# Modulation vectors: which engine multiplies and sums the gates' and the shifts' weight pieces

## The chip, the cores and the metric

One core of a Trainium2 chip runs the whole network. It has a matrix engine (TensorE, PE), a vector engine (VectorE, DVE), an activation engine (ScalarE, ACT), a general engine (GpSimd, POOL) and a queue that issues the DMAs (SyncE, SP). The metric is the device time of one execution in microseconds (us).

## The reference

Three kinds of layer follow one another: a hybrid attention layer with a dense feed-forward, a state-space layer (Mamba) with a mixture of experts, and two attention layers of a second block. Six times the normed activations are modulated by a vector that is computed from a conditioning vector `c` of 1024 numbers:

```
def adaln(c, w, b):
    mod = jax.nn.silu(c) @ w + b
    shift, scale, gate = jnp.split(mod[:, None, :], 3, axis=-1)
    return shift, scale, gate

def modulate(x, norm_w, shift, scale):
    return rmsnorm(x, norm_w) * (1 + scale) + shift
```

Each `w` is 1024 x 3072 in float32, 12.6 MB. The shift and the scale are needed at the layer's norm, the gate only at the layer's end, where it multiplies what is added to the residual.

## The kernel before

**The stream.** All weights come from memory in chunks of at most 128x1024 float32 (512 KB), through a ring of six buffers (`RING`). The DMA queue fills buffer c % 6 when chunk c-6 has been used up. There are two kinds of chunk. A *half* is a piece of a matrix that TensorE multiplies: ScalarE rounds it (line 507), VectorE subtracts the rounded part from the raw one (line 519, both inputs in SBUF), and TensorE takes three products of high and low parts (lines 530 to 532); the ring buffer is free after VectorE's subtraction. A *piece* belongs to a modulation: 24 of them for each of the six, `step` 0 to 15 (even ones the shift's, odd ones the scale's columns) and `gate` 16 to 23.

**What is done with a piece.** VectorE multiplies it by silu(c), one number for each partition, and adds it to the accumulator `macc`, 128x1024 for each of shift, scale and gate: the first piece of each with one product (line 580), the others with a product and a sum in one instruction (line 583). The ring buffer is free after it. When all pieces of a vector are summed, TensorE sums the partitions with matmuls against a matrix of ones (`mod{i}.sum` after step 15, `mod{i}.gates` after gate 23), and VectorE adds the bias (lines 589 to 603). Of modulation 0, TensorE multiplies pieces 9 and 10 directly (`DIRECT`), so that VectorE does 142 of the 144.

**What sets the order.** Every engine's instructions stand in an order written out by hand. The list `Stream.back` gives the pieces' order; `back_steps` and `back_until` take the next entries of it between the halves, at the same places of VectorE's and TensorE's programs. Modulation 0 runs at the very start, its gates and modulation 1 in the hybrid layer (one piece after each half), modulations 2, 3 and most of 4 in the dense feed-forward and the first part of the Mamba layer; then there is a pause (`BACK_PAUSE`) through the experts, and the last gates of 4 and all of 5 come in the first layer of the second block. Semaphore counts are found by a rehearsal of the same programs, and named: `mod1.step23` is the event that gate piece 23 of modulation 1 is in the sum. GpSimd does nothing.

Of the kernel before, what the change touches and what calls it, by code (L numbers as in the profile page):

```python
# [12 lines left out]
ALU = mybir.AluOpType  # L13
# [3 lines left out]
D = 1024  # L17
T = 256
NT = 2
KD = 8  # L20
# [46 lines left out]
class Ledger:  # L67
# [8 lines left out]
    def tick(self, sem, name, by=1):  # L76
        n = self.reached.get(sem.name, 0) + by
        self.reached[sem.name] = n
        self.brought[name] = (sem, n)
        return sem, by  # L80

    def when(self, name):
        return (None, 1) if self.known is None else self.known[name]
# [19 lines left out]
class Banks:  # L103
# [35 lines left out]
SEMAPHORES = (  # L139
    "params_landed", "x_landed", "x_scaled", "tables_landed", "start_landed", "raw_landed0", "raw_landed1", "raw_landed2", "raw_landed3", "raw_landed4", "raw_landed5",  # L140
    "half_rounded", "half_split", "half_used", "vector_step", "scalar_step",
    "mod_stepped", "mod_summed", "mod_ready", "small_split",
    "squared", "weighted", "norm_scaled", "norm_rooted", "norm_turned", "norm_filled_a", "norm_filled_v", "h_rounded", "h_split",
    "row_spread", "row_copied", "mix_turned", "mix_rounded", "mix_split", "added",
    "proj_out_a", "proj_out_v", "proj_turned",
# [318 lines left out]
def landed(k, key):  # L464

    c = k.stream.chunk_of[key]
    return k.landed[c % RING], 16 * (c // RING + 1), k.ring[c % RING]
# [5 lines left out]
def on_sync(sp, k):  # L473

    S, d = k.S, k.d
    sp.dma_start(k.par[:, :], d["par"]).then_inc(S.params_landed, 16)
    sp.dma_start(k.X[:, :, :], d["x"].rearrange("(t p) n -> p t n", p=128)).then_inc(S.x_landed, 16)
    for c, (src, width, freed) in enumerate(k.stream.chunks):
        if c == RING:
            sp.dma_start(k.cst[:, 0:512], d["cst"][:, 0:512]).then_inc(S.tables_landed, 16)  # L480
        if c == 2 * KD + RING:
            for dst, src_ in ((k.cst[:, 512:], d["cst"][:, 512:]), (k.small[:, :], d["small"]), (k.postok[:, :], d["pos"]),
                              (k.dtw[:, :, :], d["dtw"])):
                sp.dma_start(dst, src_).then_inc(S.start_landed, 16)
        if c == k.stream.chunk_of["half", k.stream.first["second0"]] + SPLITS + RING:
            over_sync(sp, k)
        if c >= RING:
            sp.wait_ge(*k.when(k.stream.chunks[c - RING][2]))
        sp.dma_start(k.ring[c % RING][:, 0:width], src).then_inc(k.landed[c % RING], 16)
    for t in range(NT):  # L490
        for c in range(2):
            sp.wait_ge(*k.when(f"s1.added{2 * t + c}"))
            sp.dma_start(k.out[t * 128:(t + 1) * 128, c * 512:(c + 1) * 512], k.X[:, t, c * 512:(c + 1) * 512]).then_inc(S.out_landed, 16)
    sp.wait_ge(S.out_landed, 64)
# [40 lines left out]
def mm(pe, out, a, b, start=True, stop=True):  # L535
    return pe.matmul(out, a, b, start=start, stop=stop, skip_group_check=True)  # L536
# [11 lines left out]
def mod_col(i):  # L548
    return 16 + (8 if i >= 4 else 0)
# [4 lines left out]
DIRECT = (10, 9)  # L554


def back_vector(v, k):

    if k.at_back["vector"] == len(k.stream.back):
        return  # L560
    kind, i, r = k.stream.back[k.at_back["vector"]]
    k.at_back["vector"] += 1
    if kind in ("rest", "shift"):
        return
    S, tick, when = k.S, k.tick, k.when
    mod, bias = k.d["mod"][i], k.V[f"b{i}"]
    if kind in ("step", "gate"):
        k.stream.ask(("mod", i, r), mod[r], QUARTER, f"mod{i}.step{r}")
        if i == 0 and r in DIRECT:
            return  # L570
        sem, value, w = landed(k, ("mod", i, r))
        n, part, before = (r // 2, r % 2, r - 2) if kind == "step" else (r - 2 * KD, 2, r - 1)
        if i == 0 and before in DIRECT:
            before -= 2
        c = k.st[:, mod_col(i) + n:mod_col(i) + n + 1]
        m = k.macc[:, part * D:(part + 1) * D]
        v.wait_ge(sem, value)
        if n == 0:
            v.wait_ge(*when("c.silu" if i == 0 else f"mod{i - 1}.sum" if kind == "step" else f"mod{i - 1}.gates"))
            v.tensor_scalar(m, w[:, :], c, None, ALU.mult).then_inc(*tick(S.mod_stepped, f"mod{i}.step{r}"))  # L580
        else:
            v.wait_ge(*when(f"mod{i}.step{before}"))
            v.scalar_tensor_tensor(out=m, in0=w[:, :], scalar=c, in1=m, op0=ALU.mult, op1=ALU.add).then_inc(*tick(S.mod_stepped, f"mod{i}.step{r}"))  # L583
    elif kind == "sum":
        bank = k.banks[k.bank_of.get(f"mod{i}.sum", 0)]
        m = k.mods[:, i, 8:16]
        if i == 0:
            v.wait_ge(*when(f"mod0.step{DIRECT[-1]}"))
            v.tensor_tensor(k.mods[:, 0, 0:16], k.banks[k.bank_of.get("mod0.direct", 0)][:, 0:16], bias[:, 0:16], ALU.add).then_inc(*tick(S.mod_ready, "mod0.biased"))
            v.wait_ge(*when("mod0.biased"))  # L590
            bias = k.mods[:, 0, :]
        v.wait_ge(*when(f"mod{i}.sum"))
        v.tensor_tensor(k.mods[:, i, 0:16], bank[:, 0:16], bias[:, 0:16], ALU.add).then_inc(*tick(S.mod_ready, f"mod{i}.summed"))
        v.wait_ge(*when(f"mod{i}.summed"))
        v.scalar_tensor_tensor(out=m, in0=m, scalar=1.0, in1=k.V[f"n{i}"], op0=ALU.add, op1=ALU.mult).then_inc(*tick(S.mod_ready, f"mod{i}.ready"))
    else:
        bank = k.banks[k.bank_of.get(f"mod{i}.gates", 0)]
        m = k.mods[:, i, 16:24]
        v.wait_ge(*when(f"mod{i}.gates"))
        v.tensor_tensor(m, bank[:, 16:24], bias[:, 16:24], ALU.add).then_inc(*tick(S.mod_ready, f"mod{i}.{'gated' if i < 4 else 'biased'}"))  # L600
        if i >= 4:
            v.wait_ge(*when(f"mod{i}.biased"))
            v.tensor_tensor(m, m, k.V[f"post{i - 4}"], ALU.mult).then_inc(*tick(S.mod_ready, f"mod{i}.gated"))


def back_tensor(pe, k):
    if k.at_back["tensor"] == len(k.stream.back):
        return
    kind, i, r = k.stream.back[k.at_back["tensor"]]
    k.at_back["tensor"] += 1  # L610
    if i == 0 and kind == "step" and r in DIRECT:
        direct_tensor(pe, k, r)
    if kind in ("step", "gate", "rest"):
        return
    if i == 0 and kind in ("shift", "sum"):
        first_sum_tensor(pe, k, kind)
        return
    lo, hi, steps = (0, 16, f"mod{i}.step15") if kind == "sum" else (16, 24, f"mod{i}.step23")
    bank = k.back_banks.borrow(pe, f"mod{i}.{kind}" if kind == "sum" else f"mod{i}.gates", f"mod{i}.summed" if kind == "sum" else f"mod{i}.gated")
    pe.wait_ge(*k.when(steps))  # L620
    for j in range(lo, hi):
        last = mm(pe, bank[:, j:j + 128], k.macc[:, j * 128:(j + 1) * 128], k.C["ones"])
    last.then_inc(*k.tick(k.S.mod_summed, f"mod{i}.sum" if kind == "sum" else f"mod{i}.gates"))
# [267 lines left out]
def square(a, k, name, t, c, into):  # L891

    a.activation(into, k.X[:, t, c * 512:(c + 1) * 512], ACT.Square,
                 accum_out=k.st[:, 56 + 2 * t + c:57 + 2 * t + c]).then_inc(*k.tick(k.S.squared, f"{name}.squared{2 * t + c}"))
# [2487 lines left out]
def on_scalar(a, k):  # L3382
    S, tick, when = k.S, k.tick, k.when
    a.wait_ge(S.params_landed, 16)
    a.activation(k.st[:, 0:16], k.par[:, 0:16], ACT.Exp, scale=-1.0).then_inc(*tick(S.scalar_step, "c.exp"))
    a.wait_ge(S.x_landed, 16)
    for t in range(NT):
        for c in range(2):
            if t == 1:
                a.wait_ge(*when(f"x.squared{c}"))  # L3390
            square(a, k, "x", t, c, k.arena[:, c * 512:(c + 1) * 512])
    hybrid_scalar(a, k)
    dense_scalar(a, k)
    mamba_scalar(a, k)
    moe_scalar(a, k)
    final_scalar(a, k)
    for l in range(2):
        second_scalar(a, k, l)


def model(nc, d, out):
    with ExitStack() as ctx:
        k = Kernel(nc, ctx, d, out)
        k.start_over()
        for program in (on_vector, on_scalar, on_tensor, on_sync):
            program(Rehearsal(), k)
        k.ledger.close()
        k.start_over()
        with nc.Block() as block:
            block.tensor(lambda e: on_tensor(e, k))  # L3410
            block.vector(lambda e: on_vector(e, k))
            block.scalar(lambda e: on_scalar(e, k))
            block.sync(lambda e: on_sync(e, k))


# [145 lines left out]
```

## Time and profile before

| | |
|---|---|
| median of 3 runs | 2034.95 us (2033.78 to 2046.62) |
| profiled execution, its own time | 2032.43 us |
| span of its trace | 2030.7 us |
| TensorE busy | 96% of the span |
| VectorE busy | 1701.1 us (84%) |
| ScalarE busy | 1323.5 us (65%) |
| GpSimd busy | 0.2 us |
| moved by DMA | 560 MB, mean 276 GB/s |

The busy share of TensorE is that of overlapping, modelled spans: it says when the engine had work, not that it ran at its peak. "Waits" name the engine and line that stood still, the one that released it, the sum in us, how often and the longest.

### The profile page before, as it was taken

The page shows a single profiled execution, that of the slowest core. Times are in us where ns is not written, and L with a number is a line of the kernel's source. Part 1 is how long each engine was busy: PE and PEld are TensorE (multiplying, and loading weights), DVE is VectorE, ACT ScalarE, POOL GpSimd, SP SyncE. Part 2 cuts the span into 40 slices and gives each one's busy share as a digit, 9 for nine tenths or more (in the row PEclk, how much of TensorE's full clock was granted, in tenths as well). Part 3 has the DMA queues.
Part 4 walks back from the last instruction along what each step waited for, and adds up shares of the span by engine and source line. Part 5 has one row for each costly group of instructions (what it writes and reads, how often), then busy time and mean ns, then how long its engine had stood idle before and what let it go on. Part 6 is the DMA issues. An engine that isn't in the chain of part 4 may idle for free.

```text
span 2030.7 us, 28448 instructions
## 1 busy us (share of the span) xinstructions
PE 1951.6 (96%) x10304; PEld 1630.0 (80%) x10304; DVE 1701.1 (84%) x2491; ACT 1323.5 (65%) x1976; POOL 0.2 (0%) x4
## 2 busy tenths in 40 slices
PE   6898999998998999999999999999999998999997
PEld 5777889978977788788888878888888786787886
DVE  7797878768886698989989899898989998986864
ACT  4453544355674687778888787887878785455553
POOL 0000000000000000000000000000000000000000
PEclk9998999999999999999999999999999999999999
DMA  9856689845332298989989899898999994873630
GB/s 371 311 193 232 244 300 329 285 146 193 142 111 98 104 376 326 365 327 387 366 338 374 323 367 382 330 368 328 374 359 351 353 387 157 291 250 114 229 131 25
DMA packets 154211, 560.20 MB, mean 276 GB/s; under 512 B 17232, under 2 KB 17488, under 8 KB 153936
## 3 DMA queue, kind: packets, MB, share of 16 engines
q1 hardware_dynamic: 154064, 558.30, 74.8%
q8 instruction: 85, 1.39, 0.3%
q14 instruction: 62, 0.51, 0.1%
HBM read 557.18 MB, written 1.05 MB: 275 GB/s over the span
## 4 chain that ended last, share of the span: by engine, by line
PE 80%; DVE 10%; ACT 5%; issue 3%; DMA 2%; SPq 0%; DVEq 0%; ACTq 0%
PE ps L530 22%; PE ps L532 22%; PE ps L531 22%; PE ps L536 10%; PE ps L540 3%; DVE spl L519 2%; DVE macc L583 2%; ACT sph L507 2%; DMA ring<-in_mod 1%; DMA ring<-in_hyb_w_in 1%; DVE arena L2177 1%; DMA ring<-in_dense_down 1%; ACT arena L774 1%; ACT arena L2143 1%; DVE hL L887 0%
## 5 line engine op out<-in xcount | busy, mean ns | idle before, releaser
L519 DVE TENSOR_TENSOR spl<-ring,sph 128x1024 fp32r<-128x1024 f32 x906 | 1076.4, 1217 | 185.5 <-ACT sph L507 173.1
L507 ACT ACTIVATE sph<-ring 128x1024 fp32r<-128x1024 f32 x906 | 948.5, 1058 | 392.5 <-PE ps L532 214.3
L530 PE MATMUL ps<-sph,hH 128*128 128x512 f32 (+1 forms) x1296 | 518.2, 400 | 2.5 <-DVE hL L887 1.3
L532 PE MATMUL ps<-sph,hL 128*128 128x512 f32 (+1 forms) x1296 | 505.2, 390 | 0.0
L531 PE MATMUL ps<-spl,hH 128*128 128x512 f32 (+1 forms) x1296 | 504.1, 389 | 0.0
L530 PEld LDWEIGHTS ps<-sph,hH 128*128 128x128 f32 x1296 | 244.0, 188 | 52.2 <-issue 3.8
L532 PEld LDWEIGHTS ps<-sph,hL 128*128 128x128 f32 x1296 | 243.5, 188 | 51.6
L531 PEld LDWEIGHTS ps<-spl,hH 128*128 128x128 f32 x1296 | 244.1, 188 | 47.7 <-issue 1.0
L530 PE MATMUL ps<-sph,rH 128*128 128x512 f32 x664 | 268.4, 404 | 4.2 <-DVE rL L1237 3.2
L532 PE MATMUL ps<-sph,rL 128*128 128x512 f32 x664 | 259.9, 391 | 0.0
L531 PE MATMUL ps<-spl,rH 128*128 128x512 f32 x664 | 259.3, 391 | 0.0
L530 PE MATMUL ps<-hH,sph 128*128 128x256 f32 x640 | 186.3, 291 | 5.9 <-DVE arena L1193 4.0
L531 PE MATMUL ps<-hL,sph 128*128 128x256 f32 x640 | 183.4, 287 | 0.0
L532 PE MATMUL ps<-hH,spl 128*128 128x256 f32 x640 | 183.3, 286 | 0.0
L583 DVE SCALAR_TENSOR_TENSOR macc<-ring,st,macc 128x1024 f32<-128x1024 f32 x124 | 158.1, 1278 | 3.5 <-DMA ring<-in_mod 2.3
L530 PEld LDWEIGHTS ps<-sph,rH 128*128 128x128 f32 x664 | 125.1, 188 | 32.4 <-DVE rL L1237 4.0
L536 PE MATMUL ps<-arena 128*128 128x128 f32 (+6 forms) x828 | 137.6, 307 | 9.8 <-DVE arena L2336 7.1
L532 PEld LDWEIGHTS ps<-sph,rL 128*128 128x128 f32 x664 | 124.9, 188 | 27.3
L531 PEld LDWEIGHTS ps<-spl,rH 128*128 128x128 f32 x664 | 125.4, 189 | 24.7 <-issue 1.0
L540 PEld LDWEIGHTS ps<-cst,arena 128*128 128x128 f32 (+1 forms) x636 | 82.8, 145 | 67.0 <-issue 34.1
L530 PEld LDWEIGHTS ps<-hH,sph 128*128 128x128 f32 x640 | 125.3, 196 | 8.6 <-DVE arena L1193 4.2
L540 PE MATMUL ps<-cst,arena 128*128 128x128 f32 (+1 forms) x636 | 109.9, 281 | 22.2 <-ACT arena L2161 5.5
(316 smaller groups left out, 1702.6 us busy)
## 6 DMA issues: line engine op xcount, KB each, us to landing
ring<-in_moe_gu SPq DMA_DIRECT2D x448, 512.0 KB, 5.3
ring<-in_moe_down SPq DMA_DIRECT2D x224, 512.0 KB, 5.3
ring<-in_mod SPq DMA_DIRECT2D x144, 512.0 KB, 5.2
ring<-in_w_in SPq DMA_DIRECT2D x64, 512.0 KB, 4.4
ring<-in_dense_gu SPq DMA_DIRECT2D x44, 512.0 KB, 5.3
ring<-in_ssm_w_in SPq DMA_DIRECT2D x40, 512.0 KB, 3.8
ring<-in_dense_down SPq DMA_DIRECT2D x22, 512.0 KB, 5.5
ring<-in_hyb_w_in SPq DMA_DIRECT2D x20, 512.0 KB, 5.7
```

The lines of the kernel that those rows point to most:

```text
L507: a.activation(k.high[m % SPLITS][:, 0:w], raw[:, 0:w], ACT.Copy).then_inc(k.S.half_rounded, 1)
L519: v.tensor_tensor(k.low[m % SPLITS][:, 0:w], raw[:, 0:w], k.high[m % SPLITS][:, 0:w], ALU.subtract).then_inc(*k.tick(k.S.half_split, f"hal ...
L530: pe.matmul(out, a[0], b[0], start=start, stop=False, skip_group_check=True)
L531: pe.matmul(out, a[0], b[1], start=False, stop=False, skip_group_check=True)
L532: return pe.matmul(out, a[1], b[0], start=False, stop=stop, skip_group_check=True)
L536: return pe.matmul(out, a, b, start=start, stop=stop, skip_group_check=True)
L540: return pe.transpose(out, in_, k.C["ident"][0:n, 0:n])
L583: v.scalar_tensor_tensor(out=m, in0=w[:, :], scalar=c, in1=m, op0=ALU.mult, op1=ALU.add).then_inc(*tick(S.mod_stepped, f"mod{i}.step{r}"))
L774: a.activation(k.norm_space.fulls[2 * t + h][:, j, :], bank[:, j * 128:(j + 1) * 128], ACT.Identity, bias=k.mods[:, i, c:c + 1], scale=k.m ...
L2143: a.activation(conv_slot(k, f), bank, ACT.Identity, bias=k.V["convb"][:, f:f + 1], scale=cw[:, f, 3:4]).then_inc(*tick(S.conv_in, f"ssm{j} ...
L2177: v.scalar_tensor_tensor(out=dst, in0=M.raw[m % 6][:, n:n + T], scalar=cw[:, f, n:n + 1], in1=dst, op0=ALU.mult, op1=ALU.add).then_inc(*ti ...
```

## The change

GpSimd gets a program of its own. It takes the gates' pieces of all six modulations (48) and, from modulation 1 on, the shifts' pieces (the even steps, 40): 88 of the 142 that VectorE did. VectorE keeps modulation 0's steps and all scales. For the first piece of a vector GpSimd does one product into `macc`; for each of the others a product in place in the ring buffer, a wait for that product and for the sum before, and a sum into `macc`. The ring buffer is free after the sum. TensorE's matmuls for `mod{i}.sum` wait for the last shift piece as well as for the last scale piece. The pieces' order, the ring and TensorE's program are otherwise the same.

```
+def pooled(kind, i, r):
+
+    return kind == "gate" or kind == "step" and i > 0 and r % 2 == 0
+
+
+def back_pool(g, k, i, r):
...
+    c, m = k.st[:, mod_col(i) + n:mod_col(i) + n + 1], k.macc[:, part * D:(part + 1) * D]
+    g.wait_ge(sem, value)
+    if n == 0:
+        g.wait_ge(*when("c.silu" if i == 0 else f"mod{i - 1}.sum" if kind == "step" else f"mod{i - 1}.gates"))
...
+        g.tensor_scalar(m, w[:, :], c, None, ALU.mult).then_inc(*tick(S.mod_pooled, f"mod{i}.step{r}"))
+        return
+    g.tensor_scalar(w[:, :], w[:, :], c, None, ALU.mult).then_inc(*tick(S.mod_scaled, f"mod{i}.scaled{r}"))
+    g.wait_ge(*when(f"mod{i}.scaled{r}"))
+    g.wait_ge(*when(f"mod{i}.step{before}"))
+    g.tensor_tensor(m, m, w[:, :], ALU.add).then_inc(*tick(S.mod_pooled, f"mod{i}.step{r}"))
...
 def back_vector(v, k):
...
         k.stream.ask(("mod", i, r), mod[r], QUARTER, f"mod{i}.step{r}")
-        if i == 0 and r in DIRECT:
+        if i == 0 and r in DIRECT or pooled(kind, i, r):
             return
...
     pe.wait_ge(*k.when(steps))
+    if kind == "sum":
+        pe.wait_ge(*k.when(f"mod{i}.step14"))
```

Three places show what it moves. The first is VectorE's program at the end of the hybrid layer's attention: line 519 is a half, lines 580 and 583 pieces of modulation 1, lines 676 to 684 the Newton step of the GLA heads' norm. Before:

```order
L519 TENSOR_TENSOR spl<-ring,sph 128x1024
L583 SCALAR_TENSOR_TENSOR macc<-ring,st,macc 128x1024
L1711 COPY arena<-ps 128x512
L583 SCALAR_TENSOR_TENSOR macc<-ring,st,macc 128x1024
L580 TENSOR_SCALAR macc<-ring,st 128x1024
L1420 TENSOR_SCALAR st<-st 128x8
L583 SCALAR_TENSOR_TENSOR macc<-ring,st,macc 128x1024 x2
L676 RECIPROCAL st<-st 128x8
L678 TENSOR_TENSOR st<-st 128x8
L680 TENSOR_TENSOR st<-st 128x8
L682 TENSOR_SCALAR st<-st 128x8
L684 TENSOR_TENSOR st<-st 128x8
```

The same place in the change, where later lines have moved by 34 and line 583 is now 615:

```order
L519 TENSOR_TENSOR spl<-ring,sph 128x1024
L1745 COPY arena<-ps 128x512
L615 SCALAR_TENSOR_TENSOR macc<-ring,st,macc 128x1024
L1454 TENSOR_SCALAR st<-st 128x8
L710 RECIPROCAL st<-st 128x8
L712 TENSOR_TENSOR st<-st 128x8
L714 TENSOR_TENSOR st<-st 128x8
L716 TENSOR_SCALAR st<-st 128x8
L718 TENSOR_TENSOR st<-st 128x8
```

Four of five pieces have left VectorE here: shift piece 14 and gate pieces 16 to 18 of modulation 1.

The second place is VectorE's program in the dense feed-forward, at the end of modulation 2 (lines 1842 and 1847 are the feed-forward's own work). Before:

```order
L519 TENSOR_TENSOR spl<-ring,sph 128x1024
L1842 TENSOR_TENSOR arena<-arena,ps 128x256 x2
L1847 TENSOR_TENSOR rL<-arena,rH 128x256 x2
L519 TENSOR_TENSOR spl<-ring,sph 128x1024
L583 SCALAR_TENSOR_TENSOR macc<-ring,st,macc 128x1024 x2
L519 TENSOR_TENSOR spl<-ring,sph 128x1024
L580 TENSOR_SCALAR macc<-ring,st 128x1024
L519 TENSOR_TENSOR spl<-ring,sph 128x1024
L583 SCALAR_TENSOR_TENSOR macc<-ring,st,macc 128x1024
L519 TENSOR_TENSOR spl<-ring,sph 128x1024
```

In the change, the same stretch:

```order
L615 SCALAR_TENSOR_TENSOR macc<-ring,st,macc 128x1024
L519 TENSOR_TENSOR spl<-ring,sph 128x1024 x3
L1876 TENSOR_TENSOR arena<-arena,ps 128x256 x2
L1881 TENSOR_TENSOR rL<-arena,rH 128x256 x2
L519 TENSOR_TENSOR spl<-ring,sph 128x1024
```

What is left on VectorE between the pieces of the scale is almost only line 519, with both inputs in SBUF.

The third is GpSimd, whose program before has four small memsets and nothing else. In the change it begins like this (modulation 0's gates; the name `ring` is that of the six buffers):

```order
L575 TENSOR_SCALAR macc<-ring,st 128x1024
L577 TENSOR_SCALAR ring<-ring,st 128x1024
L580 TENSOR_TENSOR macc<-macc,ring 128x1024
L577 TENSOR_SCALAR ring<-ring,st 128x1024
L580 TENSOR_TENSOR macc<-macc,ring 128x1024
```

In all GpSimd has 11 rows of line 575, 77 of line 577 and 77 of line 580, and VectorE 110 rows fewer than before (merged rows count once).

## Rows read from the trace of the kernel before

**Rows 1.** The page's first part, and of its second the slices of VectorE and GpSimd.
```profile
PE 1951.6 (96%) x10304; PEld 1630.0 (80%) x10304; DVE 1701.1 (84%) x2491; ACT 1323.5 (65%) x1976; POOL 0.2 (0%) x4
...
DVE  7797878768886698989989899898989998986864
...
POOL 0000000000000000000000000000000000000000
```

**Rows 2.** The table by stretches: length, busy us of each engine, granted clock, DMA share, GB/s.
```profile
40.00:160.00 120.00, 112.35 (x759) 92.32 (x759) 99.23 (x203) 62.28 (x145) 0.00 (x0) 0.97 0.70 248
160.00:185.00 25.00, 19.05 (x125) 16.79 (x124) 24.15 (x43) 7.99 (x20) 0.00 (x0) 0.80 0.68 229
185.00:222.00 37.00, 35.30 (x189) 28.36 (x188) 27.73 (x50) 18.43 (x34) 0.00 (x0) 1.00 0.51 177
222.00:400.00 178.00, 175.47 (x1290) 167.24 (x1289) 139.33 (x164) 74.47 (x101) 0.00 (x0) 1.00 0.88 314
400.00:440.00 40.00, 37.39 (x183) 28.16 (x182) 24.29 (x59) 20.33 (x40) 0.00 (x0) 0.96 0.24 86
440.00:480.00 40.00, 36.56 (x293) 36.22 (x292) 35.50 (x47) 23.54 (x45) 0.00 (x0) 0.96 0.83 284
...
1728.00:1760.00 32.00, 31.23 (x147) 25.31 (x146) 30.63 (x57) 17.11 (x32) 0.00 (x0) 1.00 0.88 317
1760.00:1830.00 70.00, 70.00 (x376) 57.29 (x375) 60.84 (x129) 38.99 (x84) 0.00 (x0) 1.00 0.71 246
...
1890.00:1906.00 16.00, 15.63 (x74) 12.68 (x72) 15.76 (x31) 5.80 (x6) 0.00 (x0) 1.00 0.88 336
```

**Rows 3.** The same table for `macc`'s instructions on VectorE alone: length, busy (count), clock.
```profile
222.00:400.00 178.00, 56.39 (x47) 1.00 0.88 314
```

**Rows 4.** Who waited for whom, TensorE, three stretches; then the DMA queue, whole span.
```profile
PE ps L530 <- DVE arena L1193: 4.0, 1, 4.0
...
PE ps L540 <- DVE arena L1758: 2.5, 1, 2.5
PE ps L540 <- DVE arena L1432: 2.0, 1, 2.0
PE ps L530 <- DVE rL L1237: 1.5, 1, 1.5
...
PE ps L536 <- DVE arena L1842: 2.5, 2, 2.2
...
SPq L489 <- DVE macc L583: 114.9, 120, 5.9
```

**Rows 5.** The chain in order of time, 155 to 184 us: start, us, what.
```profile
159.35 1.28 DVE macc L583
...
163.19 1.29 DVE macc L583
164.58 1.28 DVE macc L583
...
175.77 1.28 DVE macc L583
```

**Rows 6.** TensorE in order of time, before and behind the clock's return.
```profile
178.90 0.63 PE L531 MATMUL ps<-spl,rH 128*128 128x512 f32 x1
...
182.33 0.39 PE L532 MATMUL ps<-sph,rL 128*128 128x512 f32 x1
182.56 1.95 PE L536 MATMUL ps<-cst,macc 128*128 128x128 f32 x16
```

**Rows 7.** Groups: passes over a 128x1024 tile on VectorE and ScalarE.
```profile
L519 DVE TENSOR_TENSOR spl<-ring,sph 128x1024 fp32r<-128x1024 f32 x906 | 1076.4, 1217 | 185.5 <-ACT sph L507 173.1
L507 ACT ACTIVATE sph<-ring 128x1024 fp32r<-128x1024 f32 x906 | 948.5, 1058 | 392.5 <-PE ps L532 214.3
...
L583 DVE SCALAR_TENSOR_TENSOR macc<-ring,st,macc 128x1024 f32<-128x1024 f32 x124 | 158.1, 1278 | 3.5 <-DMA ring<-in_mod 2.3
```

**Rows 8.** Instructions that write `macc`: one line's count, ns min/median/max, first and last start.
```profile
L580 DVE TENSOR_SCALAR macc<-ring,st x18: 741/746/754, 8.0 to 1824.9; 128x1024 f32<-128x1024 f32 x18
```

More of the change, by code:

```diff
@@ L141 @@
     "half_rounded", "half_split", "half_used", "vector_step", "scalar_step",
-    "mod_stepped", "mod_summed", "mod_ready", "small_split",
+    "mod_stepped", "mod_pooled", "mod_scaled", "mod_summed", "mod_ready", "small_split",
     "squared", "weighted", "norm_scaled", "norm_rooted", "norm_turned", "norm_filled_a", "norm_filled_v", "h_rounded", "h_split",
@@ L554, with on_gpsimd @@
 DIRECT = (10, 9)
+def pooled(kind, i, r):
+    return kind == "gate" or kind == "step" and i > 0 and r % 2 == 0
+def back_pool(g, k, i, r):
+    S, tick, when = k.S, k.tick, k.when
+    sem, value, w = landed(k, ("mod", i, r))
+    kind, n, part, before = ("step", r // 2, 0, r - 2) if r < 2 * KD else ("gate", r - 2 * KD, 2, r - 1)
+    c, m = k.st[:, mod_col(i) + n:mod_col(i) + n + 1], k.macc[:, part * D:(part + 1) * D]
+    g.wait_ge(sem, value)
+    if n == 0:
+        g.wait_ge(*when("c.silu" if i == 0 else f"mod{i - 1}.sum" if kind == "step" else f"mod{i - 1}.gates"))
+        if (kind, i) == ("gate", 4):
+            g.wait_ge(*when("ssm.added3"))
+        if (kind, i) == ("step", 5):
+            g.wait_ge(*when("final.weighted3"))
+        g.tensor_scalar(m, w[:, :], c, None, ALU.mult).then_inc(*tick(S.mod_pooled, f"mod{i}.step{r}"))
[4 more added lines that the diff above has]
+    g.tensor_tensor(m, m, w[:, :], ALU.add).then_inc(*tick(S.mod_pooled, f"mod{i}.step{r}"))
+def on_gpsimd(g, k):
+    for kind, i, r in k.stream.back:
+        if pooled(kind, i, r):
+            back_pool(g, k, i, r)
 def back_vector(v, k):
@@ L3404, in model @@
         k.start_over()
-        for program in (on_vector, on_scalar, on_tensor, on_sync):
+        for program in (on_vector, on_scalar, on_tensor, on_gpsimd, on_sync):
             program(Rehearsal(), k)
@@ L3412, in model @@
             block.scalar(lambda e: on_scalar(e, k))
+            block.gpsimd(lambda e: on_gpsimd(e, k))
             block.sync(lambda e: on_sync(e, k))
```

## Prediction

> **What bounds the kernel now.** I read the page's first part, then the table by stretches, then who waits for whom, then the chain in the places where TensorE stood still. The page says that TensorE has work for 96% of the span, VectorE for 84%, GpSimd for nothing [rows 1]. The pieces stand in two regions only, 8 to 480 us and 1728 to 1906 us; in the experts between them the change touches nothing. By stretches [rows 2] TensorE is the bound nearly everywhere: in the dense feed-forward (222 to 400) it is busy for 175.5 of 178 us with VectorE at 139.3, and from 1760 to 1830 for all 70 us. Over the nine stretches shown TensorE is idle for 558 - 533 = 25 us. That is the most that can be won there by taking work off VectorE, apart from the granted clock, which is below 1.00 in four of them, 0.80 from 160 to 185.
>
> Where TensorE waits for VectorE, the waits are few [rows 4]: 4.0 us at 52, then 2.5, 2.0 and 1.5 us at the end of the hybrid attention, and 2.5 us in two waits in the dense part. At the end of the attention the chain goes through the pieces themselves [rows 5]: they stand in VectorE's program between the steps of the heads' norm that TensorE needs. The reader should see that a busy VectorE is not a bound by itself: it has 39 us of idle time in the dense stretch, but little to spare in four others (24.2 of 25, 35.5 of 40, 30.6 of 32, 15.8 of 16).
>
> **What is removed.** 77 products with a sum and 11 single products leave VectorE: 77 x 1.278 [rows 7] + 11 x 0.746 [rows 8] = 106.6 us of instructions, nearly 1.2 us a piece. All but a few of them lie beside TensorE's work and are worth nothing by themselves. What lies on the path: at 52 us a part of the 4.0 us wait, since VectorE no longer stands behind the landing of gate pieces before it copies what TensorE waits for (I take 3); at 160 to 178 the three waits of 6.0 us, before which six pooled pieces stand, behind them ScalarE's and TensorE's own steps come next, so I take 4; the clock of that place, where matmuls take 0.63 instead of 0.39 us [rows 6] for about 3 us, I take 1.5; in the dense part 1.5 of 2.5; in the Mamba part and the second block, where TensorE is idle for 3.4 and 1.1 us, 2. Together 12 us. The order fences show that the other engines' programs stay as they are, and the ring is asked for the same chunks in the same order. DMA, products of TensorE and VectorE's bias steps cost nothing more. The added wait of TensorE for shift piece 14 is satisfied when GpSimd keeps up, since that piece comes one before scale piece 15.
>
> **What is added.** 88 products and 77 sums on GpSimd. No row shows GpSimd at arithmetic. The nearest are the passes of the other engines over the same tile [rows 7, 8]: VectorE 0.746 us with one input and 1.217 with two, ScalarE 1.058 with one. The lower end is thus 0.75 + 1.22 = 1.97 us for a piece; as the upper end I take twice that, 3.9. I take ScalarE's 1.06 for each tile read, so 1.06 for the product and 2.12 for the sum, 3.2 us for a piece: I expect an engine that nobody used for this to be nearer to the slow rows than to the fast one, and this is above the middle. In the dense stretch 32 of the 47 pieces [rows 3] go over, one in 5.6 us: GpSimd alone keeps up with that at either end. The Trainium skill (GPSIMD Engine Reference, Performance versus the Vector engine) gives 4497 ns for a two-input float32 sum of 2048 elements; half of it would be an estimate of 2.2 us for the sum here, and the total would move by some 8 us. No row here shows it.
>
> **Whether the two engines work side by side** decides the sign, and no row tells, since none has both at work. One end: they don't disturb each other, and GpSimd's 88 x 3.2 = 280 us cost nothing. The other: whenever both read SBUF, one stands still until the other's instruction is done. What then decides is that VectorE's remaining work is mostly line 519, with both inputs in SBUF, so there is little beside which GpSimd could run. Taken in turns, a piece uses 3.2 us of the pair's time where it used 1.28: 1.9 us more. By stretches, with the pooled pieces counted along the list of pieces against the starts of lines 580 and 583 [rows 2]:
>
> 40 to 160: 16 pieces, 99.2 + 30.4 = 129.6 of 120 us, 10 over. 160 to 185: 10 pieces, 43.2 of 25, 18 over. 222 to 400: 32 pieces, 139.3 + 60.8 = 200.1 of 178, 22 over. 440 to 480: 4 pieces, 43.1 of 40, 3 over. 1728 to 1760: 10 pieces, 49.6 of 32, 18 over. 1760 to 1830: 8 pieces, 76.0 of 70, 6 over. 1890 to 1906: 5 pieces, 25.3 of 16, 9 over. 185 to 222 and 400 to 440 have one piece each and room to spare, and one falls at 1833.
>
> That is 86 us, the upper end for this case. It is too much, for two reasons: in the attention stretches most of VectorE's time is not line 519 but small instructions or ones that read PSUM, beside which GpSimd can run, and a surplus can be worked off in the idle stretch that follows, as long as the ring and the split halves (six each) hold out. I take a third to a half of the surplus in these stretches, 5 + 6 + 8 + 3 + 3, and nearly all in the dense part, where the remaining work is line 519, 18 + 1: 44 us. It doesn't matter which engine gives way. If VectorE does, its subtractions come late and TensorE waits for halves; if GpSimd does, it must live on VectorE's gaps, which in the dense stretch are 178 - (139 - 41) = 80 us for 32 x 3.2 = 102 us, and then its ring buffers come free late and the halves behind them land late. The DMA queue already waits 114.9 us for pieces [rows 4], mostly unfelt.
>
> The Trainium skill (SBUF — State Buffer, Who interferes with whom) says that a VectorE instruction with two SBUF inputs contends with a GpSimd instruction that reads SBUF, and that the later one is blocked for the whole of the other: it speaks against this change, and by it the sum is the one in turns. Without that rule my estimate would be 12 us less time instead of 44 more. No row of this trace bears it out or refutes it.
>
> **The cases.** (A) In turns: 2034.95 + 44 = 2079 us, 2055 to 2121 by the bounds of 20 and 86 us. For it speaks the high load of VectorE in just the stretches with the pieces; against it, that the trace has no such collision to show. Any shorter GpSimd time helps: at 1.97 us a piece the same sums leave 15 us of surplus, and some 2043 us. At 3.9 they give 147 us, and with half of it relieved some 2110. The case turns from slower to no change where a pair of GpSimd instructions takes under 2.6 us (36 us of surplus, about 20 left). Chance 0.52. This is the forecast.
>
> (B) Side by side: GpSimd runs ahead of VectorE, buffers come free early, and only the waits of 12 us go: 2023 us, 2010 to 2033. For it speaks that every wait named above has a pooled piece before it; against a larger gain, the 25 us of idle time in all. Chance 0.30.
>
> (C) Side by side, but GpSimd late where TensorE needs it. TensorE stands at `mod1.gates` at 182.6 us [rows 6], in the middle of the hybrid output's product, and everything of TensorE is queued behind that wait. GpSimd has some 32 us (from the landing of piece 14 at about 150) for ten pieces: 32 us at 3.2 us a piece, no margin; at 3.9, 39 us, so 7 late, and the same order again at modulation 4's gates after the pause. The 12 us are eaten up: 2035, 2028 to 2042. Chance 0.13. The remaining 0.05 is for a GpSimd far slower than 3.9 us a piece, over 2121 us.
>
> That the change doesn't do what it says can be left out: GpSimd's program has 11 + 77 + 77 instructions, and VectorE's has lost as many pieces.
>
> **The numbers.** The trace's execution took 2032.43 us (2030.7 of span and 1.7 around it), 2.5 below the median; I add the differences to the median. One per cent, 20 us, is about what a measurement of this kernel can tell from no change. Faster than that is only B's tail: 0.06. Within: most of B, C, and the mild end of A: 0.41. Slower: the rest of A and the last case: 0.53. Since the signs are mixed, the range must reach from B to A's upper part: 2015 to 2112 us; A's own is 2055 to 2121.
>
> **What the profile after would show.** If A is right: line 519's mean above 1217 ns, with single ones of 3 us or more, or sums on GpSimd far longer than the product and uneven; VectorE nearly full from 222 to 400; ScalarE and TensorE waiting for line 519 there, and that stretch some 18 us longer. If B is right: line 519 still at 1.22 us, VectorE busy for some 100 us less, the waits for lines 1758 and 1432 gone, the clock from 160 to 185 above 0.80 and the dense stretch unchanged. C shows as a wait of TensorE for GpSimd at `macc`. I am wrong if VectorE's instructions keep their durations beside GpSimd, or if GpSimd's pair is under 2.6 us.

## The result, and the profile after

The changed kernel takes 2124.81 us (median of 4 runs, 2119.52 to 2125.67); the kernel before, with the run made beside it, 2037.02 us. The ratio is 1.0432, with a 95% interval of 1.0411 to 1.0454: 4.3% or 88 us slower. The profiled execution took 2125.18 us, with a span of 2123.3 us, 92.6 us more than before.

The page's first part, and of its second the slices of VectorE, of GpSimd and of the granted clock (before: [rows 1]):

```profile
PE 1977.7 (93%) x10304; PEld 1651.4 (78%) x10304; DVE 1741.6 (82%) x2403; ACT 1325.2 (62%) x1976; POOL 501.4 (24%) x169
...
DVE  7597777757778688998989899898989998696764
...
POOL 1859498973000000000000000000000002961500
PEclk9898999999999999999999999999999999899999
```

GpSimd is busy for 501 us where the prediction had 280, and in the slices of the dense stretch it is nearly full. VectorE lost 106.6 us of instructions and is busy for 40 us more than before. The page's groups, the line's last field being idle time before it (before: [rows 7, 8]):

```profile
L519 DVE TENSOR_TENSOR spl<-ring,sph 128x1024 fp32r<-128x1024 f32 x906 | 1138.7, 1286 | 221.9 <-ACT sph L507 208.2
...
L575 POOL TENSOR_SCALAR macc<-ring,st 128x1024 f32<-128x1024 f32 x11 | 41.0, 3726 | 1276.9 <-DMA ring<-in_mod 1276.9
L577 POOL TENSOR_SCALAR ring<-ring,st 128x1024 f32<-128x1024 f32 x77 | 257.8, 3349 | 217.5 <-DMA ring<-in_mod 217.4
...
L580 POOL TENSOR_TENSOR macc<-macc,ring 128x1024 f32<-128x1024 f32 x77 | 203.5, 2643 | 6.4
```

A product takes 3.35 us and a sum 2.64: 6.0 us for a piece instead of the 3.2 that I took, and 1.5 times my upper end. Line 519's mean rose from 1217 to 1286 ns, so that both things which the prediction looked for are there: VectorE is stopped, and GpSimd is slow. Which of them costs the time, the profile alone doesn't say. TensorE's busy time rose by 26.1 us for the same 10304 matmuls, at a mean granted clock of 0.971 instead of 0.988. The 88 us hold this part too; it is not a third cause, as the run with six memsets below has it as well (0.970, 1975.2 us busy).

How a stop looks: VectorE, then GpSimd, in order of time, in the dense stretch:

```profile
300.21 0.17 DVE L625 TENSOR_TENSOR mods<-ps,par 128x16 f32<-128x16 f32 x1 [1.12 <-PE ps L536]
300.42 1.85 DVE L627 SCALAR_TENSOR_TENSOR mods<-mods,par 128x8 f32<-128x8 f32 x1
...
311.94 2.10 DVE L3034 TENSOR_TENSOR cs<-cs 128x16 f32<-128x16 f32 x1 [0.39 <-ACT cs L3043]
```
```profile
299.83 2.42 POOL L580 TENSOR_TENSOR macc<-macc,ring 128x1024 f32<-128x1024 f32 x1
302.23 2.85 POOL L577 TENSOR_SCALAR ring<-ring,st 128x1024 f32<-128x1024 f32 x1
...
311.61 2.41 POOL L580 TENSOR_TENSOR macc<-macc,ring 128x1024 f32<-128x1024 f32 x1
```

Line 627 works on eight numbers for each partition. It takes 0.17 us elsewhere, and here 1.85: it ends at 302.27, where the sum beside it ends (299.83 + 2.42 = 302.25). The other pair shows the same (314.04 and 314.02). The stop lasts to the end of the sum, however small VectorE's instruction. Not every instruction is stopped: line 625, with one input in PSUM (the matrix engine's result memory), ran beside the same sum in its usual 0.17 us.

How lateness looks: the DMA queue's and TensorE's waits for GpSimd (before: [rows 4]).

```profile
SPq L489 <- DVE spl L519: 1366.3, 856, 30.2
SPq L489 <- POOL macc L580: 236.6, 57, 5.9
...
PE ps L536 <- POOL macc L580: 12.0, 2, 8.7
```

The queue that fills the ring waits 236.6 us for GpSimd's sums; before, it waited 114.9 us for VectorE's pieces. Over all lines that work on pieces, GpSimd's and VectorE's, that is 311.6 us after and 124.3 before. At the end of the hybrid layer the chain runs through GpSimd alone, pair after pair (start, us, what; compare [rows 5]):

```profile
184.08 2.83 POOL ring L577
186.91 0.07 issue
186.98 2.58 POOL macc L580
189.56 2.87 POOL ring L577
...
192.50 2.34 POOL macc L580
```

By stages, from the starts of line 989, 2288 and 2941's instructions on VectorE (first sum into the residual, first of the Mamba scan, final norm) in each trace:

| stage | before | after | difference |
|---|---|---|---|
| start to the hybrid layer's first sum | 198.2 | 230.0 | +31.8 |
| to the Mamba scan (the dense stretch lies here) | 311.8 | 346.0 | +34.2 |
| scan and experts, no pieces in them | 1189.5 | 1190.3 | +0.8 |
| final norm to the last sum of the second block | 326.9 | 353.8 | +26.9 |

### The profile page after: what moved, and what is told of

It is laid out like the page before. It is cut to its first block, busy times and chain, and to the rows that moved or that the text cites. A ratio compares the mean times of both kernels' runs of the same rounds, so it can differ in the third digit from the quotient of the medians.

```text
span 2123.3 us, 28527 instructions
## 1 busy us (share of the span) xinstructions
PE 1977.7 (93%) x10304; PEld 1651.4 (78%) x10304; DVE 1741.6 (82%) x2403; ACT 1325.2 (62%) x1976; POOL 501.4 (24%) x169
## 4 chain that ended last, share of the span: by engine, by line
PE 61%; POOL 16%; DVE 8%; issue 7%; ACT 4%; DMA 3%; SPq 0%; DVEq 0%; ACTq 0%; POOLq 0%
PE ps L530 17%; PE ps L532 17%; PE ps L531 17%; POOL ring L577 8%; PE ps L536 8%; POOL macc L580 7%; DVE spl L519 3%; PE ps L540 3%; POOL macc L575 2%; ACT sph L507 2%; DMA ring<-in_mod 1%; DVE arena L2211 1%; DMA ring<-in_moe_gu 1%; DVE macc L615 1%; DVE arena L3330 1%
## 5 line engine op out<-in xcount | busy, mean ns | idle before, releaser
L519 DVE TENSOR_TENSOR spl<-ring,sph 128x1024 fp32r<-128x1024 f32 x906 | 1138.7, 1286 | 221.9 <-ACT sph L507 208.2
L575 POOL TENSOR_SCALAR macc<-ring,st 128x1024 f32<-128x1024 f32 x11 | 41.0, 3726 | 1276.9 <-DMA ring<-in_mod 1276.9
L577 POOL TENSOR_SCALAR ring<-ring,st 128x1024 f32<-128x1024 f32 x77 | 257.8, 3349 | 217.5 <-DMA ring<-in_mod 217.4
L580 POOL TENSOR_TENSOR macc<-macc,ring 128x1024 f32<-128x1024 f32 x77 | 203.5, 2643 | 6.4
L536 PE MATMUL ps<-arena 128*128 128x128 f32 (+6 forms) x828 | 142.9, 315 | 19.6 <-DVE arena L1736 10.2
```

Source lines behind the costliest of these rows:

```text
L519: v.tensor_tensor(k.low[m % SPLITS][:, 0:w], raw[:, 0:w], k.high[m % SPLITS][:, 0:w], ALU.subtract).then_inc(*k.tick(k.S.half_split, f"hal ...
L575: g.tensor_scalar(m, w[:, :], c, None, ALU.mult).then_inc(*tick(S.mod_pooled, f"mod{i}.step{r}"))
L577: g.tensor_scalar(w[:, :], w[:, :], c, None, ALU.mult).then_inc(*tick(S.mod_scaled, f"mod{i}.scaled{r}"))
L580: g.tensor_tensor(m, m, w[:, :], ALU.add).then_inc(*tick(S.mod_pooled, f"mod{i}.step{r}"))
```

## The experiments

Theory 1: GpSimd's reads stop VectorE, and the stops cost the time. Theory 2: a piece takes GpSimd so long that ring buffers and sums are late, and the lateness costs it. Most experiments change one of the two alone. Every time is compared with runs of the kernel before on the same chip.

**Prices of single instructions.** The kernel before, with this GpSimd program beside the experts and again at the end. VectorE's pieces after the pause wait for the twelfth memset:

```
+    dst, src, c = k.macc[:, 2 * D:3 * D], k.macc[:, D:2 * D], k.st[:, 16:17]
...
+        lambda: g.tensor_scalar(dst, src, c, None, ALU.mult),
+        lambda: g.tensor_scalar(dst, src, 0.5, None, ALU.mult),
+        lambda: g.tensor_tensor(dst, src, k.macc[:, 2 * D:3 * D], ALU.add),
+        lambda: g.tensor_copy(dst, src),
+        lambda: g.memset(dst, 0.0),
...
+    for place, event, n in (("beside", "ssm.added3", 12), ("alone", "s1.added3", 3)):
...
```

> The kernel before, with a GpSimd program on which nothing depends, on two thirds of macc that nobody uses during the experts: 12 products by a per-partition scalar, 12 by a constant, 12 sums of two tiles, 12 copies and 12 memsets, all 128x1024, beside VectorE's work in the experts; and 3 of each at the very end, when VectorE has nothing left to do. The end stage adds some 35 us that say nothing. Theory 1 (the engines block each other): beside VectorE the kinds that read take clearly longer than alone, by up to one VectorE instruction, 1.2 us, and line 519 has single instructions of 2.5 us and more in that stretch, but not beside the memsets. Theory 2 (GpSimd is slow by itself): alone a product takes about as long as in the change, 3.2 us, and a sum 2.5 us, and line 519 keeps its 1.22 us.

It ran once, in 2099.73 us; the time itself answers neither theory. GpSimd in order of time, the five kinds beside VectorE (12 each), then alone (3 each):

```profile
676.32 38.70 POOL L562 TENSOR_SCALAR macc<-macc,st 128x1024 f32<-128x1024 f32 x12 [675.88 <-DVE X L1017]
715.10 40.24 POOL L563 TENSOR_SCALAR macc<-macc 128x1024 f32<-128x1024 f32 x12
755.42 38.22 POOL L564 TENSOR_TENSOR macc<-macc 128x1024 f32<-128x1024 f32 x12
793.70 23.68 POOL L565 COPY macc<-macc 128x1024 f32<-128x1024 f32 x12
817.44 12.10 POOL L566 MEMSET macc<- 128x1024 f32 x12
2066.68 8.72 POOL L562 TENSOR_SCALAR macc<-macc,st 128x1024 f32<-128x1024 f32 x3 [1237.14 <-DVE X L3305]
2075.49 8.47 POOL L563 TENSOR_SCALAR macc<-macc 128x1024 f32<-128x1024 f32 x3
2084.04 7.17 POOL L564 TENSOR_TENSOR macc<-macc 128x1024 f32<-128x1024 f32 x3
2091.28 3.24 POOL L565 COPY macc<-macc 128x1024 f32<-128x1024 f32 x3
2094.58 2.97 POOL L566 MEMSET macc<- 128x1024 f32 x3
```

VectorE's subtraction of a half (line 519, here 520) in the stretches beside constant products, sums, copies, memsets, and after them (busy, mean ns):

```profile
L520 DVE TENSOR_TENSOR spl<-ring,sph 128x1024 fp32r<-128x1024 f32 x24 | 37.7, 1631 | 0.0
L520 DVE TENSOR_TENSOR spl<-ring,sph 128x1024 fp32r<-128x1024 f32 x11 | 31.7, 2938 | 0.0
L520 DVE TENSOR_TENSOR spl<-ring,sph 128x1024 fp32r<-128x1024 f32 x13 | 25.9, 2055 | 0.0
L520 DVE TENSOR_TENSOR spl<-ring,sph 128x1024 fp32r<-128x1024 f32 x9 | 11.4, 1303 | 0.0
L520 DVE TENSOR_TENSOR spl<-ring,sph 128x1024 fp32r<-128x1024 f32 x30 | 35.5, 1219 | 3.2 <-ACT sph L508 2.8
```

For one instruction, alone and beside: the product 2.9 and 3.2 us, the sum 2.4 and 3.2, the copy 1.1 and 2.0, the memset 1.0 and 1.0. Both theories hold something: the price is mostly GpSimd's own (5.3 us for a pair with nobody beside it), and the reading kinds stop VectorE. But they stop it unequally. Beside twelve sums eleven subtractions are 1.7 us longer each; beside twelve products, 24 are 0.4 longer, 0.8 us for a product; beside the memsets they are as always (the 1303 holds one that began beside a copy).

**The gates alone.** `pooled`, which says what GpSimd takes, returns `kind == "gate"`.

> The change with the gates' 48 pieces on GpSimd and the shifts' 40 back on VectorE. Theory 1: the loss goes with the number of pairs, 88 x 48/88 = 48 us. Theory 2: in the dense stretch GpSimd now has 16 pairs of 6 us for 178 us and is hidden; what remains is the run of eight gates at the end of the hybrid layer, at the second block's start and around 1890, 20 to 30 us in all, and the dense stretch is within 3 us of before.

2096.84 us, ratio 1.0281 (1.0255 to 1.0307), 57 us. Neither number was met: theory 1 said 48, theory 2 at most 30. The stretch to the Mamba scan was 332.4 us, 20.6 above before, where theory 2 had the dense part within 3 us: the gates' runs of eight are not hidden there either.

**GpSimd beside the dense stretch, with no ring buffer and no sum depending on it.** The kernel before, with 32 pairs more; VectorE keeps all pieces. Only the Mamba layer's first norm waits for the last pair, whose memory it needs.

```
+    places = [("step", 2, r) for r in range(6, 16, 2)] + [("gate", 2, r) for r in range(16, 24)] + ...
+    for kind, i, r in places:
+        g.wait_ge(*when(f"mod{i}.step{r}"))
+        g.tensor_scalar(a, b, c, None, ALU.mult)...
+        g.tensor_tensor(b, b, a, ALU.add)...
```

> The kernel before, VectorE keeping all pieces, and in the dense stretch alone 32 pairs of product and sum on GpSimd over spare memory of the arena, each pair starting when VectorE has done the piece that it stands for. No ring buffer, no sum and no matmul waits for GpSimd. Theory 1: VectorE is stopped as in the change, about 1.1 us for a pair, 35 us on top of 139 of 178 us, and the stretch grows by 10 to 25 us. Theory 2: nothing depends on GpSimd, so the time stays within 3 us of before.

2086.39 us, ratio 1.0240 (1.0221 to 1.0259): 49 us for 32 pairs. The last ended at 466.9 us, and the norm behind it began at 468.8: no row shows a wait for GpSimd. Theory 2's expectation failed, and theory 1's 10 to 25 us was far too low. The table by stretches, 222 to 400 us, beside the row of the kernel before in [rows 2]:

```profile
222.00:400.00 178.00, 146.18 (x1044) 139.31 (x1042) 164.79 (x130) 59.31 (x82) 155.43 (x45) 0.93 0.73 247
```

In the same 178 us TensorE does 1044 matmuls instead of 1290, while VectorE is busy for 164.8 us with 130 instructions instead of 139.3 with 164. VectorE's busy time in the whole run rose by 75.1 us (1776.2 against 1701.1), 2.3 us for a pair. So stops alone can cost 49 us, 1.5 us of time for a pair, where VectorE still has all of its own work. In the change it has 41 us less there.

**Products without sums.** The sum is left out: `macc` keeps only a first piece, and the modulations are not the reference's.

```
-    g.tensor_scalar(w[:, :], w[:, :], c, None, ALU.mult).then_inc(*tick(S.mod_scaled, f"mod{i}.scaled{r}"))
-    g.wait_ge(*when(f"mod{i}.scaled{r}"))
     g.wait_ge(*when(f"mod{i}.step{before}"))
-    g.tensor_tensor(m, m, w[:, :], ALU.add).then_inc(*tick(S.mod_pooled, f"mod{i}.step{r}"))
+    g.tensor_scalar(w[:, :], w[:, :], c, None, ALU.mult).then_inc(*tick(S.mod_pooled, f"mod{i}.step{r}"))
```

> The change with GpSimd's sums left out (macc's gates and shifts then hold only their first piece, so the modulations are wrong): a piece costs GpSimd one product of about 3.2 us instead of 5.9. Theory 2: GpSimd then has 280 us of work and keeps up nearly everywhere, and the time falls to between 2035 and 2050. Theory 1: with the sums, which read two tiles, about half of the stops go, and the time is near 2080.

2025.72 us, ratio 0.9936 (0.9913 to 0.9959): 12 us faster than before. Both expectations were too high, theory 1's by 54 us, theory 2's by 9. A product of 3.2 us is hidden, and it hardly stops VectorE (busy for 1634.7 us, against 1609 in the short hold below: 0.3 us for a product).

**Late, and nearly without stops.** Each piece is six memsets of `macc` on GpSimd; products and sums are left out, and gates and shifts are zero. The hold is the change's 6 us, except that the 11 first pieces, one product there, are held some 2 us longer.

```
-    g.tensor_scalar(w[:, :], w[:, :], c, None, ALU.mult)...
-    g.tensor_tensor(m, m, w[:, :], ALU.add)...
+    for j in range(HOLD):
+        g.memset(m, 0.0).then_inc(*tick(S.mod_scaled, f"mod{i}.scaled{r}.{j}"))
+        g.wait_ge(*when(f"mod{i}.scaled{r}.{j}"))
+    g.memset(m, 0.0).then_inc(*tick(S.mod_pooled, f"mod{i}.step{r}"))
```

> The change with each of GpSimd's 88 pieces replaced by six memsets of macc, one after the other, about 6 us in all: the piece's product and sum are left out (the gates and shifts are zero), but the ring buffer is held, and the sums are late, as in the change. GpSimd reads nothing, and the first experiment showed line 519 at its own 1.22 us beside memsets. Theory 1 (VectorE stopped by GpSimd's reads is what costs): nothing is stopped, 2015 to 2040 us. Theory 2 (6 us for a piece is too long for the ring and for the matmuls that wait): most of the loss is there, 2090 to 2125 us.

2118.46 us, ratio 1.0409 (1.0391 to 1.0426). Line 519, and the waits of the DMA queue and of TensorE for GpSimd:

```profile
L519 DVE TENSOR_TENSOR spl<-ring,sph 128x1024 fp32r<-128x1024 f32 x906 | 1077.0, 1217 | 315.9 <-ACT sph L507 304.7
```
```profile
SPq L489 <- POOL macc L583: 338.4, 76, 6.7
...
PE ps L536 <- POOL macc L583: 27.2, 3, 18.0
```

No subtraction is stopped (1217 ns), VectorE stands idle before them for 316 us (241.8 with two memsets, below), and 85 of the change's 88 us are there. Memsets are not quite free of stops, though. VectorE beside them:

```profile
314.46 0.96 DVE L3026 TENSOR_SCALAR cs<-cs 128x16 f32<-128x16 f32 x1
```

The same instruction takes 0.17 us with two memsets. Fifteen such `TENSOR_SCALAR` and one cast are longer in this run, by 8 us together, and VectorE is busy for 1614.6 us against 1609.1 with two memsets. Next to the change's stops that is little: lateness, almost alone, is enough for the whole loss.

**The same with two and with four memsets for a piece.**

> The same with two memsets for a piece, about 2 us. The control: neither late nor stopping. Both theories: no slower than the product-only run, 2010 to 2026 us; it shows the most that can be had by taking these 88 pieces off VectorE.

> As the long and the short hold, with four memsets for a piece, about 4 us, which is the upper end of the piece's price in the prediction. It cost 101 us to go from 2 to 6 us of hold (2018 to 2118). Lateness as a queue (GpSimd falls behind only where pieces come closer than it can do them: one in 3.2 us at the end of the hybrid layer, one in 5.6 on average in the dense stretch): 4 us is mostly hidden, 2025 to 2045 us. Lateness in proportion to the hold: about 2068 us.

Two: 2017.73 us, ratio 0.9918 (0.9902 to 0.9935), 16 us faster. Four: 2033.37 us, ratio 0.9997 (0.9980 to 1.0015). Both came out as expected. From 2 to 4 us of hold the time rises by 16 us, from 4 to 6 by 85: a queue that overflows, and not a cost in proportion to the hold.

**Sums without products.** Each piece is added as it is; gates and shifts are not the reference's.

```
-    g.tensor_scalar(w[:, :], w[:, :], c, None, ALU.mult).then_inc(*tick(S.mod_scaled, f"mod{i}.scaled{r}"))
-    g.wait_ge(*when(f"mod{i}.scaled{r}"))
```

> The change with GpSimd's products left out: each piece is added to macc as it is (gates and shifts wrong), one sum of 2.4 to 2.6 us that reads two tiles. Theory 1: VectorE is stopped by the sums almost as in the change, some 1.2 us a piece, which only replaces the 1.2 us taken off it; by the stops alone between 2035 and 2070. Theory 2: a piece is shorter than in the product-only run (3.2 us), so it is as fast as that one, 2020 to 2035.

2077.01 us, ratio 1.0215 (1.0198 to 1.0232). The expectation of theory 2 failed, and theory 1's upper end (2070) lay 7 us too low: a piece of 2.7 us is quicker than the product's, yet the time is 51 us more (55, each against the kernel before on its chip). VectorE's subtractions and GpSimd's sums (groups, mean ns):

```profile
L519 DVE TENSOR_TENSOR spl<-ring,sph 128x1024 fp32r<-128x1024 f32 x906 | 1119.8, 1265 | 199.6 <-ACT sph L507 186.8
```
```profile
L578 POOL TENSOR_TENSOR macc<-macc,ring 128x1024 f32<-128x1024 f32 x77 | 208.1, 2702 | 399.9 <-DMA ring<-in_mod 397.6
```

VectorE was busy for 1716.0 us, 107 more than in the short hold (the two memsets): 1.2 us of stop for a piece, and GpSimd was idle for 400 us waiting for data. Here the stops are the cause, since nothing else of the short hold changed but 0.7 us of length, and four memsets for a piece, longer still, took 2033 us.

**The shifts alone.** `pooled` returns `kind == "step" and i > 0 and r % 2 == 0`.

> The change with the shifts' 40 pieces on GpSimd and the gates' 48 back on VectorE, the complement of the gates-only run, which cost 57 us. Both theories expect less for a piece than there, since a scale piece on VectorE stands between any two of GpSimd's: theory 2 nearly nothing outside the dense stretch, 10 to 20 us in all; theory 1 some 40 us, in proportion to the pieces.

2052.90 us, ratio 1.0094 (1.0066 to 1.0122), 19 us, against 57 for the gates: 0.5 us a piece against 1.2. Theory 2's 10 to 20 us was right, theory 1's 40 was not. The gates come in runs, the shifts with a scale piece between them. VectorE is busy for 1728.5 us here and 1719.9 with the gates, and the 8.6 us are about what the eight pieces more cost that it keeps: it was stopped for about as long in both. So stops in proportion to the pieces don't explain 19 against 57, and a queue would; it wasn't shown more directly.

**Small doses.** Six pieces, the first three gate pieces of modulations 1 and 4 (`kind == "gate" and i in (1, 4) and r < 2 * KD + 3`); then those of all six modulations.

> The change with six pieces on GpSimd alone: gate pieces 16 to 18 of modulations 1 and 4, which stand on the chain at 162 to 166 and 1729 to 1735 us of the kernel before. They come three in a row with pauses, so lateness costs nothing by the queue; six pairs stop VectorE for some 10 us in all where it is busy. Theory that small doses pay: 2025 to 2032 us, a little under before. Theory that the stops eat what leaves VectorE: 2032 to 2040.

> The same for all six modulations, 18 pieces. If small doses pay, 2022 to 2032 us; if the stops eat the gain, 2034 to 2045, some 15 us above the ceiling that the short hold showed for all 88.

Six: 2041.01 us, ratio 1.0027 (1.0012 to 1.0042), 1 us above what was expected if the stops eat the gain. Eighteen: 2044.67 us, ratio 1.0048 (1.0029 to 1.0067), inside that range. No version with real sums on GpSimd beats the kernel before. In the first, the end of the hybrid attention shows a reason; VectorE in order of time, then the chain (start, us, what):

```profile
158.60 2.84 DVE L519 TENSOR_TENSOR spl<-ring,sph 128x1024 fp32r<-128x1024 f32 x1 [3.40 <-ACT sph L507]
```
```profile
161.36 2.13 DVE macc L615
...
165.29 2.25 DVE st L1454
167.56 0.22 ACT st L724
```

Three pieces of 3.2 us in all have left this chain [rows 5]. In their place shift piece 14, still VectorE's, takes 2.13 us instead of 1.28, and line 1454, which works on eight numbers, 2.25 instead of 0.16: 2.9 us of stops on the chain, and the subtraction just before is stopped for 1.6 (2.84 instead of 1.22).

## Why the prediction was wrong

**The direction and the chain of reasons.** Slower was right, and so was the ground for it, that VectorE's instructions with two inputs in SBUF are stopped by GpSimd's that read it. The size was 44 us and is 88. The step that failed is the price of a piece on GpSimd, "I take ScalarE's 1.06 for each tile read [...] 3.2 us for a piece", with 3.9 as the upper end. It is 5.3 us alone and 6.0 in the kernel. The sum was nearly right (2.12 taken, 2.4 alone); the product, with one input, takes 2.9 us where 1.06 was taken. No row of the trace before could show it, and the upper end was twice the lower end for no better reason than that. The prediction did leave 0.05 for "a GpSimd far slower than 3.9 us a piece, over 2121 us": that is what came, and it had the smallest chance of all.

**Which case it was.** By stops alone the forecast's own arithmetic gives no 88 us. A pair stops VectorE for far less than its length: VectorE's 1741.6 us after, less the 1609.1 of the short hold, where as many pieces are gone, are 132 us of stops, 1.5 us a pair and not 3.2. In the dense stretch that makes 139 - 41 + 32 x 1.5 = 146 of 178 us: it would have fitted. The row of the change for the same 1290 matmuls says so too (busy us of TensorE, its weight loads, VectorE, ScalarE, GpSimd):

```profile
253.80:449.90 196.10, 180.01 (x1290) 171.38 (x1290) 147.12 (x127) 71.41 (x98) 178.25 (x58) 0.97 0.75 266
```

"Taken in turns, a piece uses 3.2 us of the pair's time" failed twice: the pair is longer, and only some of it stands in VectorE's way. What does not fit is GpSimd itself: 32 x 6.0 = 192 us in 178, and ten pieces, 60 us, in the 32 us at the end of the hybrid layer. That is case C, with a chance of 0.13 and a price of 0 to 7 us, and the run with six memsets shows that at this length it costs 85 us with hardly a stop. Case C's own working was sound: it said that GpSimd has no margin at 3.2 and is some 7 us late at 3.9 us a piece; the run with four memsets came out as before, 16 us above the ceiling. "GpSimd alone keeps up with that at either end" in the dense stretch was true of the ends that I gave, and not of the length that it has. One more step failed: I relieved the attention stretches because of "small instructions or ones that read PSUM, beside which GpSimd can run". It holds for line 625, which reads PSUM, but the small ones in SBUF (lines 627, 3034 and 1454) are stopped for up to 2.1 us each.

**The two causes don't add.** Above the short hold (2018), stops alone cost 59 us (sums only), lateness alone 101, both together 107. A reading that fits, not shown by itself: when the ring is late, VectorE stands idle anyway, and a stop falls into time that it would have waited. Of the change's 88 us, 85 are left nearly without stops, and 43 with sums alone and 2.7 us a piece; all of the stops without the lateness was not run. The 88 us can't be divided into two parts that add up; what is shown is that each is enough to make it clearly slower.

**The smaller terms.** The gain from what leaves VectorE's path was put at 12 us; with 88 pieces gone and nearly nothing in their place it is 16, and 12 with the real products. "It doesn't matter which engine gives way" was not tested. Both give way: VectorE by 1.5 us a pair, GpSimd's pair by 0.7 us (6.0 against 5.3 alone), and by 1.6 beside the dense stretch of the kernel before (220.1 us for 32 pairs). By the Trainium skill (SBUF — State Buffer, Who interferes with whom) the later instruction is blocked for the whole of the earlier one. For the sum the trace agrees, to 0.02 us in the two pairs above; for the product it doesn't: 24 subtractions of VectorE fit beside twelve products of 3.35 us, with 0.8 us of stop for each. The measurement decides: the product stops VectorE for a quarter of its length.

**What stays open.** Whether the ring or the matmuls that wait for the sums carry the lateness was not tried apart. TensorE's own waits for GpSimd are 12.0 us of 88, the queue's 236.6, so I take it to be mostly the ring.

## What to carry to other kernels

Before work goes to an engine that is idle, its price on that engine has to be measured, alone and beside the others: an idle GpSimd took 5.3 us for what VectorE does in 1.28. Where work shares buffers in order with the critical stream, the helper's length for one piece against the shortest distance between pieces decides, and it decides as a queue does: 4 us a piece cost nothing against before, 6 us cost 85. A GpSimd sum in SBUF stops even VectorE's smallest products and sums there until it ends, as lines 627, 3034 and 1454 show, so that it is better not put beside a chain of small steps.

## What the runs showed of the hardware

- GpSimd on a 128x1024 float32 tile, with nobody beside it: product by a scalar 2.9 us (by a constant 2.8), sum of two tiles 2.4, copy 1.1, memset 1.0. The one-input product is slower than the two-input sum and 2.7 times a copy.
- Beside VectorE's subtractions: product 3.2 us, sum 3.2, copy 2.0, memset 1.0.
- A GpSimd sum held VectorE instructions of 0.16 us for up to 2.1 us, to its own end within 0.03 us. Line 625, with an input in PSUM, was not held.
- A GpSimd memset held none of VectorE's 906 subtractions (1217 ns), but some `TENSOR_SCALAR` with one SBUF input: 0.96 us instead of 0.17.
- The granted clock fell with TensorE's waits, from 0.988 over the kernel before to 0.971 in the change, and rose to 0.991 in the short hold.
